# A two-stack transformer kernel: squares of the closing norm added on VectorE, and the stick-breaking running sum as two rounded products one half later

## The reference, cut to what matters

```python
# stack 1, stick-breaking: z are the scores; keys after j and before the query are summed
w = where(mask, exp(log_sigmoid(z) + after), 0.0)      # after: minus the running sum of softplus(z)
return einsum('bhqk,bhkd->bhqd', w, vt)
...
# stack 2, end of every layer
mixed = concatenate([y_conv, y_attn, y_lru], -1) @ w_out
return _layer_norm(DEEPNORM_ALPHA * h + mixed, ln_post_g, ln_post_b)
...
def _layer_norm(x, g, b):
    mu = mean(x); var = mean(square(x - mu))
    return (x - mu) * rsqrt(var + LN_EPS) * g + b
```

## Time and profile before

| | |
|---|---|
| median of 3 runs | 3298.31 us (3298.03 to 3298.41) |
| profiled execution, its own time | 3299.16 us |
| span of that execution, first to last instruction | 3297.4 us |
| TensorE matmuls busy | 3236.8 us, 98% |
| VectorE busy | 1962.6 us, 60% |
| ScalarE busy | 1644.2 us, 50% |
| GpSimd busy | 499.9 us, 15% |
| mean granted TensorE clock | 0.991 of full |

### The profile page before, as it was taken

The page is one execution under the profiler, slowest core; times in us unless marked ns, Lnnn a source line. Parts: engine busy times, 40 slices in busy tenths (PEclk is TensorE's granted clock), DMA queues, the critical chain, the costliest instruction groups (busy, mean ns, idle before and its releaser), DMA issues.

```text
span 3297.4 us, 48068 instructions
## 1 busy us (share of the span) xinstructions
PE 3236.8 (98%) x17416; PEld 2792.9 (85%) x17416; DVE 1962.6 (60%) x2184; ACT 1644.2 (50%) x2274; POOL 499.9 (15%) x426
## 2 busy tenths in 40 slices
PE   8999999999999999999999999999988999999998
PEld 7888888888888888888888888888868999989997
DVE  5666654444444555766645545444556887568965
ACT  5445545555444445444455555444434565355743
POOL 4544500000000003554400000000002000010000
PEclk9999999999999999999999999999998999999998
DMA  6555555545555555555554554665544444444443
GB/s 229 176 173 179 172 173 173 169 167 174 188 194 194 186 199 173 184 175 169 180 177 159 173 177 160 199 195 192 185 155 155 147 144 139 163 169 150 148 160 103
DMA packets 157147, 566.90 MB, mean 172 GB/s; under 512 B 17536, under 2 KB 19728, under 8 KB 156752
## 3 DMA queue, kind: packets, MB, share of 16 engines
q1 hardware_dynamic: 155680, 558.00, 51.6%
q0 software_dynamic: 1344, 7.16, 0.6%
HBM read 562.99 MB, written 2.10 MB: 171 GB/s over the span
## 4 chain that ended last, share of the span: by engine, by line
PE 95%; DVE 2%; POOL 1%; ACT 1%; issue 0%; DMA 0%; SPq 0%; POOLq 0%; ACTq 0%; DVEq 0%
PE acc L1557 22%; PE acc L1559 22%; PE acc L1558 22%; PE acc L1808 6%; PE acc L1810 6%; PE acc L1809 6%; PE work L1617 1%; PE work L1643 1%; PE work L1787 1%; PE work L1871 1%; DVE w_lo L1004 1%; PE work L1788 1%; PE work L1789 1%; PE work L1899 0%; PE work L1628 0%
## 5 line engine op out<-in xcount | busy, mean ns | idle before, releaser
L1004 DVE TENSOR_TENSOR w_lo<-raw,w_hi 128x1024 fp32r<-128x1024 f32 x1056 | 1399.1, 1334 | 1118.1 <-ACT w_hi L600 945.8
L600 ACT ACTIVATE w_hi<-raw 128x1024 fp32r<-128x1024 f32 x832 | 876.5, 1058 | 962.6 <-PE acc L1559 961.8
L1557 PE MATMUL acc<-w_hi,hT_hi 128*128 128x512 f32 x2560 | 1015.3, 397 | 2.0 <-DVE hT_lo L1010 2.0
L1559 PE MATMUL acc<-w_hi,hT_lo 128*128 128x512 f32 x2560 | 999.1, 390 | 0.0
L1558 PE MATMUL acc<-w_lo,hT_hi 128*128 128x512 f32 x2560 | 997.5, 390 | 0.0
L1559 PEld LDWEIGHTS acc<-w_hi,hT_lo 128*128 128x128 f32 x2560 | 481.1, 188 | 102.8
L1557 PEld LDWEIGHTS acc<-w_hi,hT_hi 128*128 128x128 f32 x2560 | 481.5, 188 | 97.1 <-issue 2.4
L1558 PEld LDWEIGHTS acc<-w_lo,hT_hi 128*128 128x128 f32 x2560 | 481.9, 188 | 96.0
L614 ACT ACTIVATE w_hi<-raw 128x1024 fp32r<-128x1024 f32 x224 | 236.1, 1056 | 308.2 <-PE acc L1810 295.6
L1808 PE MATMUL acc<-h_hi,w_hi 128*128 128x272 f32 (+1 forms) x1152 | 336.5, 292 | 0.0
L1810 PE MATMUL acc<-h_hi,w_lo 128*128 128x272 f32 (+1 forms) x1152 | 329.9, 286 | 0.0
(11 more groups left out here) (303 smaller groups left out, 3618.0 us busy)
## 6 DMA issues: line engine op xcount, KB each, us to landing
raw<-weights SPq DMA_DIRECT2D x1056, 512.0 KB, 3.4
mat<-mats POOLq DMA_DIRECT2D x2, 1536.0 KB, 7.7
X<-x_in SPq DMA_DIRECT2D x8, 256.0 KB, 7.2
out<-out_rows SPq DMA_DIRECT2D x8, 256.0 KB, 2.5
par<-params POOLq DMA_DIRECT2D x2, 640.0 KB, 5.0
cst<-consts POOLq DMA_DIRECT2D x1, 704.0 KB, 4.9
cst<-consts POOLq DMA_DIRECT2D x1, 552.0 KB, 4.6
ropeC<-rope POOLq DMA_DIRECT2D x2, 256.0 KB, 5.2
```

The source lines that it names most:

```text
L600: act.activation(w_hi[:, slot, :], raw[:, slot, :], ACT.Copy).then_inc(hi_ready, 1)
L1004: dve.tensor_tensor(w_lo[:, s % RING, :], raw[:, s % RING, :], w_hi[:, s % RING, :], ALU.subtract)\
L1557: pe.matmul(o, stat[0][:, kc, token], hi, start=(kc == 0), stop=False)
L1559: ins = pe.matmul(o, stat[1][:, kc, token], hi, start=False, stop=(kc == KC - 1))
```

## The change

**Closing norm.** VectorE adds the squares of tiles 0 to 13 (in the order of `SQ_ORDER`) into `LNT[:, 0]`, 13 additions in each layer: three are called for at each of g = 105, 107, 109 and 111 (the first call only waits), two after `add_tile(14)`. TensorE's 12 products at g = 102 to 108 and those of tiles 12 and 13 go; one product of `LNT[:, 0]` takes their place in the tail, behind a new wait on `post_sqsum`. Per layer 14 products become 1.

**Running sum.** ScalarE makes a rounded copy `sm_hi` of `SM` (`softplus_hi`), VectorE the rounded rest `sm_lo`, and `cumulate` makes its two products of each head twice, with `sm_hi` and with `sm_lo`, against a rounded copy `tri` of the constants. The parts of an SB step that come after `softplus` move one half later on all three engines.

```diff
+SQ_ORDER = [0, 1, 8, 2, 3, 9, 4, 5, 10, 6, 7, 11, 12, 13]
...
+        sm_hi = mem.place("sm_hi", [P, 2, 384], F32R, at=qn_at)
+        sm_lo = mem.place("sm_lo", [P, 2, 384], F32R, at=sq_at)
...
+        tri = mem.place("tri", [P, 2 * P], F32R)
...
+                if l == 0:
+                    act.wait_ge(cst_loaded, 16)
+                    act.activation(tri[:, :], cst[:, C_NEGTRI:C_NEGTRI + 2 * P], ACT.Copy)
                 split(u, 14, 16)
...
+            def softplus_hi(m):
+
+                act.wait_ge(sp_sum, 2 * m["k"] + 2)
+                act.activation(sm_hi[:, :, :], SM[:, :, :], ACT.Copy).then_inc(sp_hi, 1)
...
-                split(u, 7, 10)
+                split(u, 7, 8)
                 if prev and prev["kind"] == "SB":
+                    softplus_hi(prev)
+                late = prev and prev["kind"] == "SB"
+                split(u, 8, 11)
+                if late:
                     stick_weights(prev)
-                split(u, 10, 12)
+                split(u, 11, 12)
...
-                split(u, 12, 15)
+                split(u, 12, 16 if late else 15)
                 if prev:
                     u_hi(prev)
-                split(u, 15, 16)
+                if not late:
+                    split(u, 15, 16)
...
+            def softplus_lo(m):
+
+                dve.wait_ge(sp_hi, m["k"] + 1)
+                dve.tensor_tensor(sm_lo[:, :, :], SM[:, :, :], sm_hi[:, :, :], ALU.subtract).then_inc(sp_ready, 1)
...
                 if prev:
-                    (mix_maps if prev["kind"] == "DA" else softplus)(prev)
-                split(u, 8, 10)
+                    (softplus if late else mix_maps)(prev)
+                if late:
+                    split(u, 8, 9)
+                    softplus_lo(prev)
+                split(u, 8 + late, 10 + late)
                 if prev:
-                    (copy_aT if prev["kind"] == "DA" else stick_args)(prev)
-                split(u, 10, 12)
+                    (stick_args if late else copy_aT)(prev)
+                split(u, 10 + late, 12)
...
+                if g in (105, 107, 109, 111):
+                    p = (g - 105) // 2
+                    for T in SQ_ORDER[3 * p:3 * p + 3]:
+                        add_squares(l, T)
                 if g == 111:
                     alpha_tile(l, 14)
                     alpha_tile(l, 15)
+
+            def add_squares(l, T):
+
+                k = FROM[l]
+                dve.wait_ge(post_sq, KC * l + SQ_MADE[T])
+                i = SQ_ORDER.index(T)
+                if i == 0:
+                    return
+                dve.wait_ge(post_sqsum, 13 * l + i - 1)
+                before = sqf[:, 0, k:TOK] if i == 1 else LNT[:, 0, k:TOK]
+                dve.tensor_tensor(LNT[:, 0, k:TOK], before, sqf[:, T, k:TOK], ALU.add).then_inc(post_sqsum, 1)
...
                 add_tile(l, 14)
+                add_squares(l, 12)
+                add_squares(l, 13)
...
                 for a in range(2):
-                    pe.matmul(work[:, 2 + a, 0:384], cst[:, C_NEGTRI:C_NEGTRI + P], SM[:, a, :], start=False, stop=True,
-                              skip_group_check=True)
-                    ins = pe.matmul(work[:, 2 + a, P:256], cst[:, C_NEGONE:C_NEGONE + P], SM[:, a, 256:384], start=False,
-                                    stop=True, skip_group_check=True)
+                    for part in (sm_hi, sm_lo):
+                        pe.matmul(work[:, 2 + a, 0:384], tri[:, 0:P], part[:, a, :], start=False, stop=True,
+                                  skip_group_check=True)
+                    for part in (sm_hi, sm_lo):
+                        ins = pe.matmul(work[:, 2 + a, P:256], tri[:, P:2 * P], part[:, a, 256:384], start=False,
+                                        stop=True, skip_group_check=True)
...
-                halves(u, hT, 3, 7, parts)
+                halves(u, hT, 3, 7 + late, parts)
                 if prev:
-                    (turn_a if prev["kind"] == "DA" else cumulate)(prev)
-                halves(u, hT, 7, 8, parts)
+                    (cumulate if late else turn_a)(prev)
+                halves(u, hT, 7 + late, 8, parts)
...
-                halves(u, hT, 8, 9)
+                halves(u, hT, 8, 9 + late)
                 if prev:
                     values(prev)
-                halves(u, hT, 9, 13)
+                halves(u, hT, 9 + late, 13 + late)
                 if prev:
                     turn_u(prev)
-                halves(u, hT, 13, 16)
+                halves(u, hT, 13 + late, 16)
...
-                if g in (102, 104, 106, 108):
-                    T = g - 102
-                    square_sum(l, T)
-                    square_sum(l, T + 1)
-                    square_sum(l, 8 + T // 2)
...
-                square_sum(l, 12)
-                square_sum(l, 13)
+                pe.wait_ge(post_sqsum, 13 * (l + 1))
+                pe.matmul(work[:, 1, FROM[l]:TOK], ones_d[:, :], LNT[:, 0, FROM[l]:TOK], start=True, stop=False)
```

More of the change, by code:

```diff
@@ L212, in build_program @@
         subln = mem.place("subln", [P, 256])
+        tri = mem.place("tri", [P, 2 * P], F32R)
+        assert mem.at <= 229376, mem.at
         x_loaded = sems("x_loaded", 8)
@@ L232, in build_program @@
             sem(n) for n in ("maxed", "probs", "mixing", "mixed", "aT_turned", "aT_copied"))
-        sp_steps, sp_ln, sp_sum, sp_ready, cumulated, w_arg, w_ready = (
-            sem(n) for n in ("sp_steps", "sp_ln", "sp_sum", "sp_ready", "cumulated", "w_arg", "w_ready"))
+        sp_steps, sp_ln, sp_sum, sp_hi, sp_ready, cumulated, w_arg, w_ready = (
+            sem(n) for n in ("sp_steps", "sp_ln", "sp_sum", "sp_hi", "sp_ready", "cumulated", "w_arg", "w_ready"))
         av_ready, o_sq, head_steps, o_rs, u_ready = (sem(n) for n in ("av_ready", "o_sq", "head_steps", "o_rs", "u_ready"))
@@ L316, in build_program @@
             sem(n) for n in ("post_delta", "post_ss", "post_var", "post_sub", "post_mul"))
-        norm_root, norm_rs = sem("norm_root"), sem("norm_rs")
+        norm_root, norm_rs, post_sqsum = sem("norm_root"), sem("norm_rs"), sem("post_sqsum")
         out_copied, out_copied2, out_stored = sem("out_copied"), sem("out_copied2"), sem("out_stored")
@@ L1086, in softplus @@
                 dve.scalar_tensor_tensor(SM[:, :, :], work[:, 2:4, 0:384], 0.0, SM[:, :, :], ALU.max, ALU.add).then_inc(sp_sum, 1)
-                dve.wait_ge(sp_sum, k + 1)
+                dve.wait_ge(sp_sum, 2 * k + 1)
                 keep = cst[:, C_SBKEEP:C_SBKEEP + 384].unsqueeze(1).to_broadcast([P, 2, 384])
-                dve.tensor_tensor(SM[:, :, :], SM[:, :, :], keep, ALU.mult).then_inc(sp_ready, 1)
+                dve.tensor_tensor(SM[:, :, :], SM[:, :, :], keep, ALU.mult).then_inc(sp_sum, 1)
+            def softplus_lo(m):
+                dve.wait_ge(sp_hi, m["k"] + 1)
+                dve.tensor_tensor(sm_lo[:, :, :], SM[:, :, :], sm_hi[:, :, :], ALU.subtract).then_inc(sp_ready, 1)
             def stick_args(m):
@@ L1120, in step @@
                     mask_scores(prev)
+                late = 1 if prev and prev["kind"] == "SB" else 0
                 split(u, 6, 8)
                 if prev:
-                    (mix_maps if prev["kind"] == "DA" else softplus)(prev)
-                split(u, 8, 10)
+                    (softplus if late else mix_maps)(prev)
[3 more added lines that the diff above has]
+                split(u, 8 + late, 10 + late)
                 if prev:
-                    (copy_aT if prev["kind"] == "DA" else stick_args)(prev)
-                split(u, 10, 12)
+                    (stick_args if late else copy_aT)(prev)
+                split(u, 10 + late, 12)
                 if this and this["kind"] == "DA":
                     qk_sums(this)
-                split(u, 12, 13)
+                split(u, 12, 13 + late)
                 if prev:
                     make_u(prev)
-                split(u, 13, 16)
+                split(u, 13 + late, 16)
                 if prev:
@@ L1905, in square_sum @@
                 pe.wait_ge(post_sq, KC * l + SQ_MADE[T])
-                return pe.matmul(work[:, 1, FROM[l]:TOK], ones_d[:, :], sqf[:, T, FROM[l]:TOK], start=(T == 0), stop=(T == 15))
+                return pe.matmul(work[:, 1, FROM[l]:TOK], ones_d[:, :], sqf[:, T, FROM[l]:TOK], start=False, stop=(T == 15))
             def after(l, g):
```

## The result

The changed kernel takes 3277.62 us (3277.45 to 3278.18, 4 runs), the one before 3298.17 us (3297.48 to 3298.41, 4 runs). The ratio is 0.9938, with a 95% interval of 0.9926 to 0.9949: 20.6 us faster, where 21.3 was forecast. The profiled execution took 3277.46 us with a span of 3275.7 us.

The account below looks back on a forecast made before the run. TensorE was taken to bound the kernel in both places: 11.6 us off the sums of squares plus 9.7 off the running sum make 21.3, so 3298.3 - 21.3 = 3277.0 us, range 3273.5 to 3285.5 us.

Parts of the forecast that it names:

- the covers: Time that feeding engines have: one half later for the running sum, the splits' lead in the ring for the closing norm.
- What bounds: TensorE, 98% of the span, sets the pace in both changed places; time taken off it comes off the end.
- Squares: Closing norm: 13 net fp32 products fewer per layer, at 0.46 and 0.43 us, save 11.6 us.
- The short rounded product: Running sum: four rounded 128-column products per `cumulate`, taken at 0.111 us each; the running sum saves 9.7 us in all.
- the nearest row: Price source for the short product: 128-column fp32 transposes of line 1617, 0.109 us each, each with its own weight load.
- Both bounds: Short product's price limits: 0.065 us from below (12.6 us saved), 0.22 us from above (2.7 us saved).
- rival 1: Running sum: a rounded 128-column product isn't shortened, 0.22 us; 14.3 us saved in all, 3284.0 us; chance 0.20.
- The cover of the running sum: `sm_lo` ready by 2035.9, TensorE asks one half later at 2037.3: 1.4 us spare, no wait.
- Rival 2: Running sum waits because `sm_lo` is late; each us beyond the spare costs 16 us; chance 0.13 together with rival 3.
- The cover of the norm: Closing norm, layer 0: VectorE takes 5.63 of TensorE's 6.04 us per pair of halves, 93%; nothing is late.
- rival 3: VectorE becomes the bound in the closing norm; whole gain there lost gives 3288.6 us; chance 0.13 together with rival 2.
- Rival 4: Running sum's new products run like fp32 ones: 27.8 us more, 3314.5 us; chance 0.05 with other ways to be slower.

Follow-up runs that it names:

- the 128 extra products: Changed kernel with each rounded 128-column product in `cumulate` issued three times, 8 more in each of 16 steps: 3291.29 us.
- the three-fold additions: Changed kernel with two idle additions beside each of VectorE's 13 additions of squares a layer: 3286.6 us.
- A shorter tail: Changed kernel with tile 14's squares also added on VectorE and TensorE making the sum of the tiles first: 3275.49 us.

## Why the prediction was right

The time, 3277.6 us, lies 0.6 us from the forecast, and the mechanism is the forecast one: TensorE is the bound, what is taken off it comes off the end, and the covers hold. Sizes that were off are named below.

- **What bounds.** TensorE's list of waits was empty at both places before and stays so; each part alone gives its products' time (10.5 and 9.1 us for 11.6 and 9.6 or so). The whole came out 0.7 us less than the sum, and the profiled execution 21.7 us below the profiled one before, 0.4 more than the sum. Both differences are smaller than the scatter in front of the norms, 1.6 to 1.9 us between executions that run the same instructions up to there. So the closeness of 0.6 us is in part luck; what the traces confirm to a tenth is the norm's part.
- **Squares.** 13 x 0.46 and 13 x 0.43 us: the chain shows 5.93 and 5.60 us.
- **The short rounded product.** The choice of the nearest row was right: 0.111 us taken, 0.107 measured by the time and 0.111 by the timeline. Both bounds fell: at 0.065 us, the line through the longer products, the 128 extra products would have cost 8.3 us, and at 0.22 us, rival 1, 28 us; they cost 13.7. Rounding shortens a product of 128 columns too, down to the pace at which the trace shows the weight loads. By the 81 ns of the Trainium skill (TensorE: Matmul & The Clock Gate, Back-to-back issue gap) the extra products would have cost, as an estimate, 10.4 us; the 13.7 measured don't agree with it.
- **The cover of the running sum.** 1.4 us of spare time were worked out, 1.5 measured. The prediction took the later half as given by the change; the runs show that it is needed exactly with the split of half 8 in the chain (20.8 us lost without it), and not needed if the rest is made at once. Rival 2's price of 16 us for each us late was a little low: a first product that starts 1.20 us late cost 1.31 a step, one that starts 1.1 late cost 1.2, which makes 17 to 18 us for each us.
- **The cover of the norm.** The load is the one worked out. VectorE's timeline in the changed kernel, two splits one pair of halves apart in layer 0:

```profile
2848.19 1.23 DVE L1023 TENSOR_TENSOR w_lo<-raw,w_hi 128x1024 fp32r<-128x1024 f32 x1 [0.81 <-ACT w_hi L620]
...
2854.25 1.23 DVE L1023 TENSOR_TENSOR w_lo<-raw,w_hi 128x1024 fp32r<-128x1024 f32 x1 [0.44 <-ACT w_hi L620]
```

Of the 6.06 us between them 0.44 are a wait, so VectorE is taken for 93%, the short gaps between its instructions counted in; in the same pair of layer 1 the wait is 0.19 of 5.68, 97% taken. It was not the bound, and rival 3 did not come up: TensorE has no wait on `w_lo`, though an odd half takes VectorE 3.41 us and TensorE 3.02. Before the splits of these halves VectorE waits between 0 and 1.1 us, where a few tenths were forecast. With the three-fold additions the excess went to the tail, not into the splits.
- **Rival 4** did not come up: each new product stands as one record.

## What to carry to other kernels

Where the bound engine has no wait at a place, price its instructions by the distance of their starts; the time of what is removed then comes off in full, as long as each new handover is checked against the time at which it is asked for. When work is moved to an engine near its limit, sum that engine's load over the stretch in which the bound engine's pace repeats, and see where an excess would surface: here it was the first product that needs the complete sum, after the last split. A rounded product of 128 columns with a weight load of its own costs about 0.11 us here, in whatever order it is issued, though its columns alone would come to 0.065. And compare two traces between marks inside the kernel before a gain of 1 or 2 us is credited to a change: here the stretch in front of the marks scattered by as much.

## What was not expected of the hardware

- A wait of TensorE costs more than its recorded idle time: 1.04 us recorded, 1.31 us lost, because the record counts from the end of the last product, 0.16 us after the next would have started, and because the first product after the wait takes 0.11 us longer until its successor.
- After a wait of 3.7 us in the tail of layer 0, fp32 products ran at 0.91 us each instead of 0.46, at a granted clock of 0.50: that is the lower of the clock's two levels, 1.2 in place of 2.4 GHz. In the changed kernel the same products followed the last half without a wait, at 0.46. So the late sum cost 2.0 us more than its lateness there, and 0.7 us more than it in layer 1, after a wait of 2.4 us. After the waits of 1.0 us at the running sum the clock stayed at 1.00.
- A shorter tail gives back part of its gain: with it the next stage's products ran at a granted clock of 0.50 for 4.8 us instead of 3.3.
